# Two trunk layers on one core: the waits of the expert weight loads, and the place of one modulation chunk

## The reference

```python
def trunk(x, cond, ...):
    for l in range(DEPTH):                                   # DEPTH = 2
        sh1, sc1, g1, sh2, sc2, g2 = modulation(cond, P['w_mod'][l], P['b_mod'][l])
        h = rmsnorm(x, P['norm1_w'][l]) * (1 + sc1) + sh1
        u_att, u_rw, u_ssd = split_cols(h @ P['w_in'][l], ...)
        o_att = attn(...)                                    # windowed attention
        o_rw  = rwkv_mixer(u_rw, ...)                        # delta-rule recurrence, both directions
        o_ssd = ssd_mixer(u_ssd, ...)                        # Mamba-2 scan, both directions
        x = x + g1 * (concat(o_att, o_rw, o_ssd) @ P['w_out'][l])
        h = rmsnorm(x, P['norm2_w'][l]) * (1 + sc2) + sh2
        x = x + g2 * moe(h, router, exp_gate[l], exp_up[l], exp_down[l])   # 16 experts, top 2 of one group

def modulation(cond, w_mod, b_mod):                          # w_mod: 1024 x 6144, float32
    return jnp.split(jax.nn.silu(cond) @ w_mod + b_mod, 6, axis=-1)
```

## Time and profile before

| | |
|---|---|
| three timed runs | 1037.3, 1035.37, 1032.6 us |
| median | 1035.37 us |
| the profiled execution | 1035.65 us |
| its span, first to last instruction | 1033.8 us |
| mean granted clock of TensorE | 0.967 |
| busy share: PE, DVE, ACT, POOL | 89, 47, 27, 6% |
| moved by DMA | 239.51 MB |

### The profile page before, as it was taken

The page is one execution under the profiler, slowest core; times in us unless marked ns, Lnnn a source line. Parts: engine busy times, 40 slices in busy tenths (PEclk is TensorE's granted clock), DMA queues, the critical chain, the costliest instruction groups (busy, mean ns, idle before and its releaser), DMA issues. The chain is left out here.

```text
span 1033.8 us, 25458 instructions
## 1 busy us (share of the span) xinstructions
PE 921.1 (89%) x11037; PEld 651.4 (63%) x11037; DVE 484.5 (47%) x1371; ACT 282.2 (27%) x655; POOL 61.8 (6%) x92
## 2 busy tenths in 40 slices
PE   7899998996799989979989999899688989997696
PEld 4455557665677875635765555766676887663365
DVE  1362288665664443112636228866686261311035
ACT  3330308433221521110143030843331161111000
POOL 0000000000000021012000000000000002000120
PEclk9899999998899999989999999999999999998999
DMA  9859624412246999999761311441206799999992
GB/s 372 359 144 277 179 82 158 171 36 93 90 178 273 422 401 347 376 378 396 320 234 60 113 46 41 154 175 37 92 10 252 309 382 326 367 374 357 391 416 81
DMA packets 43654, 239.51 MB, mean 232 GB/s; under 512 B 5136, under 2 KB 8336, under 8 KB 19984
## 3 DMA queue, kind: packets, MB, share of 16 engines
q1 hardware_dynamic: 30192, 197.42, 49.2%
q0 software_dynamic: 9504, 34.08, 10.8%
q10 hardware_dynamic: 3840, 6.29, 1.9%
HBM read 211.03 MB, written 26.74 MB: 230 GB/s over the span
## 5 line engine op out<-in xcount | busy, mean ns | idle before, releaser
L1103 PE MATMUL bank<-sb_hT,sb_ring 128*128 128x385 f32 (+1 forms) x640 | 208.9, 496 | 4.4 <-ACT sb_hT L1873 4.4
L1103 PEld LDWEIGHTS bank<-sb_hT,sb_ring 128*128 128x128 f32 (+1 forms) x640 | 116.8, 189 | 91.6 <-issue 12.1
L1873 ACT ACTIVATE sb_u<-bank 128x256 f32<-128x256 f32 (+4 forms) x136 | 58.2, 456 | 249.9 <-PE bank L1103 239.1
L1103 PE MATMUL bank<-sb_arena 64*64 64x64 f32 (+5 forms) x1032 | 96.8, 333 | 11.1 <-DMA sb_arena<-weights 6.4
L1103 PE MATMUL bank<-sb_ring,sb_arena 128*64 128x256 f32 (+4 forms) x672 | 80.9, 370 | 1.5 <-DVE sb_ring L2252 0.7
L1103 PEld LDWEIGHTS bank<-sb_arena 128*64 128x64 f32 (+2 forms) x1032 | 55.5, 145 | 38.8 <-issue 18.7
L2255 DVE SCALAR_TENSOR_TENSOR sb_xT<-bank,sb_mod,sb_xT 128x128 f32<-128x128 f32 (+1 forms) x160 | 46.4, 351 | 57.9 <-PE bank L1103 57.7
L1103 PEld LDWEIGHTS bank<-sb_ring,sb_arena 128*64 128x64 f32 (+2 forms) x672 | 56.2, 150 | 23.9 <-issue 14.6
L1103 PE MATMUL bank<-sb_u,sb_arena 64*64 64x64 f32 (+2 forms) x744 | 57.9, 325 | 12.3 <-DMA sb_u<-weights 6.5
L1103 PE MATMUL bank<-sb_o,sb_ring 128*128 128x128 f32 (+2 forms) x320 | 66.0, 361 | 0.0
L1873 ACT ACTIVATE sb_tmp<-bank 128x128 f32<-128x128 f32 x35 | 9.7, 278 | 194.1 <-PE bank L1103 194.1
(11 more groups left out here) (241 smaller groups left out, 1299.5 us busy)
## 6 DMA issues: line engine op xcount, KB each, us to landing
sb_ring<-weights SPq DMA_DIRECT2D x95, 1024.0 KB, 9.3
sb_arena<-weights SPq DMA_DIRECT2D x40, 1024.0 KB, 18.2
sb_u<-weights SPq DMA_DIRECT2D x22, 1024.0 KB, 10.8
sb_hT<-weights SPq DMA_DIRECT2D x10, 1024.0 KB, 21.5
sb_sq<-weights SPq DMA_DIRECT2D x8, 1024.0 KB, 20.3
x_slots<-sb_o POOLq DMA_DIRECT2D x1, 6912.0 KB, 40.1
sb_consts<-weights SPq DMA_DIRECT2D x6, 1024.0 KB, 23.3
sb_sq<-x_slots POOLq DMA_DIRECT2D x17, 256.0 KB, 8.1
```

Source lines behind the costliest of these rows:

```text
L1103: return nc.tensor.matmul(out, lhsT, rhs, start=start, stop=stop, skip_group_check=True)
L1873: return nc.scalar.activation(out, in_, func, **kw)
```

## The change

Two things are changed. `MOD_AT` gives two chunks to layer 0's `rw2` and none to its `norm2`. Since the chunks are dealt out in one order, `rw2` now computes chunks 9 and 10 of layer 0, `rw3` chunk 11, `ssd` chunk 0 of layer 1 and `gate` chunk 1 of layer 1, each one further on than before. And the waits of `home_free` for homes that belonged to a mixer are changed, each to another event, with the order of these loads in `homes_of` changed to follow them.

```diff
--- before.py
+++ after.py
@@ -59,7 +59,7 @@
 MOD_CHUNKS = 12
 MOD_PLACES = ["start", "norm1", "sc0", "sc2", "pv1", "pv2", "rw", "rw2", "rw3", "ssd", "gate", "norm2", "rows", "held", "tail"]
 MOD_AT = {(0, "start"): 1, (0, "norm1"): 3, (0, "sc0"): 1, (0, "sc2"): 1, (0, "pv1"): 1, (0, "pv2"): 1,
-          (0, "rw"): 1, (0, "rw2"): 1, (0, "rw3"): 1, (0, "ssd"): 1, (0, "gate"): 1, (0, "norm2"): 1, (0, "tail"): 1,
+          (0, "rw"): 1, (0, "rw2"): 2, (0, "rw3"): 1, (0, "ssd"): 1, (0, "gate"): 1, (0, "tail"): 1,
           (1, "norm1"): 1, (1, "sc0"): 1, (1, "sc2"): 1, (1, "pv1"): 1, (1, "pv2"): 1, (1, "rw"): 1,
           (1, "rw3"): 1, (1, "ssd"): 1, (1, "gate"): 1}
 
@@ -441,6 +441,7 @@
 
 KEPT = 2
 U_HOMES, ARENA_HOMES = 3, 5
+GATED_HOME = 2
 HOMES = [("ring", i) for i in range(SLOTS)] + [("u", i) for i in range(U_HOMES)] \
     + [("arena", i) for i in range(ARENA_HOMES)] + [("sq", 0), ("hT", 0), ("consts", 0)]
 
@@ -508,17 +509,27 @@
             l, after = where[1], ["u", "arena", "consts"]
         if nxt is not None and nxt[0] == "expert" and where[0] == "fixed":
             l, after = nxt[1], after + ["sq", "hT"]
-        loads += [m for m in sorted(early, key=lambda m: (HOMES[home[m]][0] in ("sq", "hT"), m)) if after and stream[m][0][1] == l and HOMES[home[m]][0] in after]
+        loads += [m for m in sorted(early, key=lambda m: (["u", "consts", "arena", "sq", "hT"].index(HOMES[home[m]][0]), m)) if after and stream[m][0][1] == l and HOMES[home[m]][0] in after]
     def free_at(n):
 
         if before[n] is not None:
             return order_of[stream[before[n]][1]]
-        l = stream[n][0][1]
-        return order_of[{"ring": ("yms", l), "sq": ("ms", l, 2, 1), "hT": ("hm", l, TILES - 1, 1)}[HOMES[home[n]][0]]]
+        l = next(m for m in range(DEPTH) if n < last_expert[m])
+        name, i = HOMES[home[n]]
+        if name == "u":
+            return max([order_of["yms", l] - 1 + (i == 2)] + [order_of["mod", *c] for c in GATE_CHUNKS if c in MOD_SCHEDULE[l, "gate"]])
+        if name == "arena":
+            return order_of["yms", l] if i == GATED_HOME else order_of["ys", l, TILES - 1, 1]
+        return order_of[{"ring": ("ys", l, TILES - 1, 1), "consts": ("gnv", l, 1), "sq": ("ms", l, 2, 1),
+                         "hT": ("hm", l, TILES - 1, 1)}[name]]
+
+    last_expert = [max(n for n in loads if stream[n][0][:2] == ("expert", l)) for l in range(DEPTH)]
 
     for l in range(DEPTH):
-        first = [n for n in loads if stream[n][0][:2] == ("expert", l) and
-                 (HOMES[home[n]][0] in ("sq", "hT", "ring") if before[n] is None else stream[before[n]][0][0] == "fixed")]
+        out_at = loads.index(next(n for n in loads if stream[n][0] == ("fixed", l, DENSE_ITEMS - 1)))
+        first = [n for n in loads[out_at + 1:] if n < last_expert[l] and
+                 (stream[n][0][:2] == ("expert", l) or stream[n][0][:2] == ("fixed", l + 1)) and
+                 (before[n] is None or stream[n][0][0] == "expert" and stream[before[n]][0][0] == "fixed")]
         at = sorted(loads.index(n) for n in first)
         assert at == list(range(at[0], at[0] + len(at)))
         loads[at[0]:at[0] + len(at)] = sorted(first, key=lambda n: (free_at(n), n))
@@ -930,8 +941,17 @@
                 elif item_before[n] is not None:
                     filled(sp, *stream[item_before[n]][1])
                 elif name == "u":
-                    filled(sp, "yms", l)
-                elif name in ("arena", "consts") or name == "ring" and n >= SLOTS + ARENA_HOMES:
+                    for c in GATE_CHUNKS:
+                        if c in MOD_SCHEDULE[l, "gate"]:
+                            filled(sp, "mod", *c)
+                    sp.wait_ge(gated_sq_ready, l + 1)
+                elif name == "consts":
+                    filled(sp, "gnv", l, 1)
+                elif name == "ring" and n >= SLOTS + ARENA_HOMES:
+                    filled(sp, "ys", l, 2, 1)
+                elif name == "arena" and i != GATED_HOME:
+                    filled(sp, "ys", l, TILES - 1, 1)
+                elif name == "arena":
                     sp.wait_ge(mix_ready, l + 1)
                 elif name == "sq":
                     filled(sp, "ms", l, 2, 1)
```

## The result

The changed kernel took 1046.59 us (median of eight runs, 1043.31 to 1055.95), the kernel before 1037.6 us in its eight. The ratio of the two is 1.0102, with a 95% interval of 1.0078 to 1.0125: slower by 1.0%, some 10.6 us. Forecast were 1042.5 us and +6.9 us over the profiled execution: the right sign, and too small.

The account below looks back on a forecast made before the run. It took the order of TensorE's work to set the end, with the DMA engines nearly level in the expert stages. Its sum 10.0 − 2.5 + 1.0 + 0.7 − 1.0 − 1.3 = +6.9 us gave 1042.5 us, range 1034 to 1047 us.

Parts of the forecast that it names:

- Step 1: Layer 0's recurrence, `rw2`: TensorE waits for chunk 10's two items, +10.0 us, with −2.5 and +1.0 us for other stops.
- the stop that falls into the stall: Layer 0's recurrence: TensorE's 2.5 us standstill after a pair of loads is absorbed by the wait at `rw2`, −2.5 us.
- The term for the stops behind the stall: Layer 0's recurrence: a similar stop may follow chunk 11's loads, partly covered by VectorE's work, +1.0 us (0 to +2.5).
- Step 2: Layer 0's recurrence, behind the stall: one more loss from TensorE's lower granted clock, +0.7 us (0 to +2).
- Rival (c): Dense work behind the `rw2` stall: the clock stays low longer, +3.4 in place of +0.7, 1045.2 us; chance 0.12.
- Step 3: Behind layer 0's second norm: taking the chunk out gains between 0.4 and 1.75 us, taken as −1.0 us.
- Step 4: Layer 0's expert stage: earlier expert loads give −1.3 us (0 to −5.3), TensorE's weight waits falling 1 to 2 us.
- Rival (a): Expert stage gives back all TensorE waits there, norm and expert gains −1.75 and −5.3 us: +2.1 us, 1037.8 us; chance 0.25.
- (b): Layer 0's recurrence: VectorE's work hides the stall and the expert stage gives its full gain, −7.05 us, 1028.6 us; chance 0.13.
- Step 5: Layer 1: its expert queue had already run out, so an earlier start changes nothing, 0 (±1) us.

Follow-up runs that it names:

- after_again: The changed kernel, unaltered, measured and profiled a second time; ratio to the kernel before 1.0114.
- chunks_only: The old kernel with the new `MOD_AT` and nothing else; ratio to the kernel before 1.0118.
- loads_only: The changed kernel with the old `MOD_AT`, so only the waits and order of the expert loads are new; ratio to the kernel before 0.9991.
- ring_turned: The changed kernel with the items of layer 1's chunks 2 and 3 in ring slots 0, 1, 3, 4, not 3, 4, 0, 1; ratio to before 1.0083.
- before_staggered: The old kernel with the second item of three pairs of chunk loads issued later; ratio to the kernel before 0.9967.
- staggered: loads_only with the second item of three pairs (chunks 9 and 10 of layer 0, 9 of layer 1) issued later; ratio to before 0.9918, repeated 0.9941.
- spread_staggered: ring_turned with layer 0's chunk 10 some 14 us later, second items of layer 0's chunks 9, 10, 11 and layer 1's 9 delayed; ratio to before 1.0044.
- both_late: staggered with both items of layer 0's chunk 9 issued between 5 and 6 us later; ratio to the kernel before 0.9949.

## Why the prediction was too small

Two readings in it were off and changed no term: by the earlier trace rows the full slices of the DMA engines are 14 to 19 and 33 to 39, and the second of its two idle times at `rw2`, 2.9 us, is 275.2 − 272.5 = 2.7 us.

**Step 1**, right in its mechanism, off in its sizes. The wait was to end at 275.2 us and ended at 274.79 us; the next step was to come 10.0 us later and came 10.4 us later. The estimate of 6.8 us for two items from the Trainium skill ("DMA: Bandwidth & Descriptors", section "Anatomy of one DMA — SWDGE (gpsimd) path"), which I set aside, was the nearer: from the first issue (267.57 us) to the start of the products of the second item (274.79 us) it is 7.2 us, not 8.5. The split was different too: 5.35 us of waiting, and not 7.7, but two chunks at a lower clock (3.64 us for chunk 9, where the old kernel took 2.63 us, and 3.86 us for chunk 10 in place of 2.2). The −2.5 us for the stop that falls into the stall was taken: the product behind it, at 274.82 us before, is at 282.87 us, 8.1 us late. Then more than that was given back. TensorE stood for 1.40 us ahead of 286.35, and three times for 0.75 to 0.93 us behind it, 3.9 us together, where the old kernel has 0.23 us of this kind between 276 and 300 us. At 300.13 us the kernel is 11.7 us behind; after_again is 11.1 us behind at the same step. I had 10.0 − 2.5 + 1.0 + 0.7 = 9.2 us. The term for the stops behind the stall, +1.0 us with an upper end of +2.5, was mis-sized: the lag grew there by 3.7 us, so VectorE's work covered none of it.

**Step 2** is in these 11.7 us. The lower clock lay in the chunks at the stall rather than behind them; from 280 us on the granted clock is 1.00. Rival (c), a longer loss in the dense work behind, did not come there. In layer 1, from 663 to 667 us, the granted clock is 0.59 behind the wait of 2.75 us in the first profile, 0.93 behind 2.68 us in after_again, and 1.00 behind 2.70 us in chunks_only. So the rule of the Trainium skill that stood beside (c) ("TensorE: Matmul & The Clock Gate", section "HAM oscillation — how this bites in real kernels") is borne out at this wait in two profiles and not in the third.

**Step 3**: 7.1 us for the norm as layer 1 showed. Of the 1.75 us gained, 1.5 us went again in the gather's products (7.14 us in place of 5.60), and up to the first home 0.5 us were left, where I took 1.0 between bounds of 0.4 and 1.75.

**Step 4** was to give 1.3 us; loads_only measured 0.9 us, within its uncertainty of nothing. The reason holds: the homes are full before the first is read, and the changed kernel's DMA engines stand idle from 379 to 382 us. But its sign for TensorE's waits does not: they were to fall by 1 to 2 us, and are 6.9 us in loads_only and 8.1 and 5.8 us in the two profiles of the changed kernel, where they were 5.3 us. Rival (a) needed this step to give 5.3 us and has fallen, (b) with it and with the stall, which nothing hid.

**Step 5, layer 1: 0 (±1), is the step that failed.** It argued from the expert loads alone and took for granted that the homes of layer 1 stayed as they were. They had turned, and one wait of 2.7 us cost 4.6 and 4.5 us with its lower clock in the two profiles, 2.9 us without it in chunks_only, and 3.2 us in the timed runs (ring_turned against after_again). With it in, my sum would have been 1045.7 to 1047.1 us. It could have been known: the homes and their last readers are fixed in the program's tables before anything runs. I read them for layer 0 alone. Together with the stops behind the stall in step 1 this is what the sum lacked.

Open: the three steps with a loss or gain add up to 11.7 − 0.5 + 4.6 = 15.8 us in the first profile, and its span is 20.3 us over that of before; the runs differ by 10.6 us. The rest, spread over the recurrence of layer 1 and the experts, differs from one execution to the next, and has no cause shown here.

## What to carry to other kernels

A step that takes buffers from a ring sets the turn of that ring for everything behind it. When such a step is added, moved or taken out, follow the slots up to the next place where only some of them may be used, however far that is, and look at whose last reader each of them now waits for. Put two steps that share a pair of buffers back to back only if the load of a pair fits between them; here a place 14 us later took away the wait's cost, and no gain of the move showed. And where TensorE runs many short instructions, try to load beside it one block at a time: that gained 0.3 to 0.8% over the kernel before in two kernels here (before_staggered, and staggered with its repetition) and nothing in a third (spread_staggered).

## What the runs showed of the hardware that I had not expected

Beside the weights (queue q1) the DMA engines carry packets that the profile calls `instruction`: 91 of them on q8 in the old kernel, 1.49 MB together, so 16 KiB each. The idle times of TensorE in the recurrence that the profile marks `issue` end a fixed time behind such a packet. The answers on DMA in the old kernel, in the two stretches 242.8 to 244.9 and 244.9 to 246 us, inside the idle time that ends at 247.25 us:

```profile
q1 hardware_dynamic: 121, 0.86, 102.0%
```

```profile
q1 hardware_dynamic: 51, 0.39, 87.3%
q8 instruction: 1, 0.02, 5.0%
```

The engines were full of weights for 2.1 us with no instruction packet among them; then one moved, and TensorE went on at 247.25 us. Searched in steps of 0.1 us, the packet ahead of each of 23 such idle times in eight traces moves 2.2 to 2.6 us before TensorE goes on:

| trace | idle time, us | packet at, us | TensorE goes on, us |
|---|---|---|---|
| before | 4.45 | 244.9 | 247.25 |
| before | 2.50 | 272.4 | 274.82 |
| staggered | 3.08 | 242.3 | 244.74 |
| staggered | 1.15 | 270.2 | 272.62 |
| both_late | 1.71 | 238.6 | 241.13 |
| changed kernel | 1.40 | 283.9 | 286.35 |

So only what is beyond some 2.4 us can have been spent on a late packet within the idle time: 2.1 us of the 4.45, and 0.1 us of the 2.50. Shorter idle times are those in which the packet moved before TensorE ran dry. That the delayed items shorten three such idle times by half, and that both_late moves them, ties them to the loads. In both_late no weights are moved from 236 to 239 us, and 1.71 us of idle time are left; by the same reading a dense stretch can outrun its instructions without any load beside it. In stretches with long products the same loads cost nothing of this kind: all idle times of this sort over 0.6 us in the old kernel lie in the two recurrences. That these packets are TensorE's instructions and wait in a queue behind the weights is my reading of this; the profile names no engine for them, and no row shows when one was asked for.
